# Modulation groups by channel quarter, and nine instead of six early w_in chunks, in the first stage of a two-block kernel

## What is computed

```python
def adaln(cvec, w, b):
    m = jax.nn.silu(cvec) @ w + b
    return jnp.split(m[:, None, :], N_MOD, axis=-1)
...
sh1, sc1, ga1, sh2, sc2, ga2 = adaln(c, w_mod[i], b_mod[i])
csh1, csc1, cga1, csh2, csc2, cga2 = adaln(c_ctx[None, :], w_mod[i], b_mod[i])
px = modulate(rms_norm(x, norm_mix[i]), sh1, sc1) @ w_in[i]
pc = modulate(rms_norm(xc, norm_mix[i]), csh1, csc1) @ w_in[i]
```

## Time and profile before

| | |
|---|---|
| median of three runs | 2884.47 us (2882.27 to 2885.92) |
| profiled execution, span | 2886.6 us (no other time of it is given) |
| PE busy | 2817.8 us, 98% |
| DVE busy | 1865.0 us, 65% |
| ACT busy | 1347.8 us, 47% |
| DMA | 532.30 MB, mean 184 GB/s |
| chain that ended last | PE 90%, DVE 4%, DMA 2%, ACT 1%, issue 1% |

### The profile page before, as it was taken

The page is one execution under the profiler, slowest core; times in us unless marked ns, Lnnn a source line. Parts: engine busy times, 40 slices in busy tenths (PEclk is TensorE's granted clock), DMA queues, the critical chain, the costliest instruction groups (busy, mean ns, idle before and its releaser), DMA issues.

```text
span 2886.6 us, 56801 instructions
## 1 busy us (share of the span) xinstructions
PE 2817.8 (98%) x24171; PEld 2382.1 (83%) x24171; DVE 1865.0 (65%) x2553; ACT 1347.8 (47%) x1947; POOL 226.0 (8%) x271
## 2 busy tenths in 40 slices
PE   6999999999999999999999999999999999999998
PEld 3687888888988878888888888888888888888887
DVE  3597886777777676664455566789775555554444
ACT  3222446566655444444444444566544444444443
POOL 1000002333231000000000000133000000000000
PEclk9999999999999999999999999999999999999999
DMA  9997881000001668876656556666556666666664
GB/s 386 369 373 262 273 274 36 8 11 10 8 8 58 209 211 261 260 236 183 189 185 194 191 180 221 189 178 182 172 182 189 191 188 188 191 189 199 189 191 160
DMA packets 470781, 532.30 MB, mean 184 GB/s; under 512 B 22920, under 2 KB 422722, under 8 KB 469634
## 3 DMA queue, kind: packets, MB, share of 16 engines
q1 hardware_dynamic: 464754, 516.13, 55.6%
q0 software_dynamic: 3408, 10.43, 1.1%
q10 hardware_dynamic: 2368, 2.11, 0.3%
HBM read 522.29 MB, written 4.19 MB: 182 GB/s over the span
## 4 chain that ended last, share of the span: by engine, by line
PE 90%; DVE 4%; DMA 2%; ACT 1%; issue 1%; ACTq 0%; SPq 0%; DVEq 0%
PE ps L2489 14%; PE ps L2500 14%; PE ps L2502 14%; PE ps L2501 14%; PE ps L2665 9%; PE ps L2490 7%; PE ps L3015 4%; PE ps L3016 2%; PE ps L2511 2%; PE ps L2512 2%; PE ps L2513 2%; DMA raw<-in_w_mod 1%; PE ps L2693 1%; PE ps L2691 1%; PE ps L2912 1%
## 5 line engine op out<-in xcount | busy, mean ns | idle before, releaser
L1596 DVE TENSOR_TENSOR lo<-raw,hi 128x1024 fp32r<-128x1024 f32 x776 | 948.5, 1228 | 714.7 <-ACT hi L1069 709.4
L1069 ACT ACTIVATE hi<-raw 128x1024 fp32r<-128x1024 f32 x776 | 820.3, 1059 | 1074.1 <-PE ps L2502 603.0
L2500 PE MATMUL ps<-hi,mov 128*128 128x512 f32 x1408 | 553.4, 393 | 3.6 <-DVE mov L1664 3.6
L2502 PE MATMUL ps<-hi,mov 128*128 128x512 f32 x1408 | 549.3, 390 | 0.0
L2501 PE MATMUL ps<-lo,mov 128*128 128x512 f32 x1408 | 549.0, 390 | 0.0
L2500 PEld LDWEIGHTS ps<-hi,mov 128*128 128x128 f32 x1408 | 264.9, 188 | 58.2 <-issue 4.4
L2502 PEld LDWEIGHTS ps<-hi,mov 128*128 128x128 f32 x1408 | 264.9, 188 | 55.9
L2501 PEld LDWEIGHTS ps<-lo,mov 128*128 128x128 f32 x1408 | 265.1, 188 | 53.9
L2489 PE MATMUL ps<-mov,hi 128*128 128x512 f32 x864 | 306.2, 399 | 0.4 <-DVE mov L2419 0.3
L2489 PE MATMUL ps<-hid,hi 128*128 128x512 f32 x704 | 244.3, 394 | 0.0
L2490 PE MATMUL ps<-mov,lo 128*128 128x256 f32 x864 | 242.2, 280 | 0.0
(11 more groups left out here) (448 smaller groups left out, 4248.7 us busy)
## 6 DMA issues: line engine op xcount, KB each, us to landing
raw<-in_w_in SPq DMA_DIRECT2D x184, 512.0 KB, 4.8
raw<-in_w_gate SPq DMA_DIRECT2D x176, 256.0 KB, 2.9
raw<-in_w_up SPq DMA_DIRECT2D x176, 256.0 KB, 3.2
raw<-in_w_down SPq DMA_DIRECT2D x88, 512.0 KB, 3.6
raw<-in_w_ffn_gate SPq DMA_DIRECT2D x176, 256.0 KB, 2.9
raw<-in_w_ffn_up SPq DMA_DIRECT2D x176, 256.0 KB, 3.1
raw<-in_w_ffn_down SPq DMA_DIRECT2D x88, 512.0 KB, 4.4
raw<-in_w_out SPq DMA_DIRECT2D x64, 512.0 KB, 4.0
```

What stands on the lines that cost most here:

```text
L1069: act.activation(hi[:, s, :, :], src, ACT.Copy).then_inc(hi_ready, 1)
L1596: dve.tensor_tensor(lo[:, s, :, :], raw_at(ph, i, j)[0], hi[:, s, :, :].bitcast(F32), ALU.subtract)\
L2500: pe.matmul(out, x(k)[:, 0, tokens], w_hi, start=first, stop=False)
L2502: mm = pe.matmul(out, x(k)[:, 1, tokens], w_hi, start=False, stop=last)
```

## The change

Each modulation group now holds shift and scale of one channel quarter: a load has two runs of 512 columns instead of one of 1024. `mod_add` adds both parts and forms the gains in each group, so `mod_ready` counts four additions per group. After group m, DVE scales the eight operands of quarter m, and ACT and DVE make their high and low parts. The early part of in_kv goes by chunk first, then by pair, so that mains 3m to 3m+2 need quarter m alone. Nine mains are early: eight among the modulation chunks (behind chunks 21 to 58), the ninth behind the last. The turns of x and ctx stand one per chunk. The loads use a list `MOD_FIRST` of twenty places, in which the later `side_hid` region serves too, and then the fourteen buffers of the ring in another order. Sides are moved from the first trip of in_kv to in_r, and the twenty of its second trip now stand behind seven mains instead of eight.

```diff
 MOD_CHUNKS = MODS * KB
-MODS_READY = 2 * MODS
-EARLY_MAINS = 6
+MOD_PARTS = 2
+MODS_READY = 2 * MOD_PARTS * MODS
+QUARTER = KB // MODS
+EARLY_MAINS = 9
-SIDES = {"in_kv": (4, 20, 20, 20), "in_lora": (8,), "in_r": (4, 4), "in_rest": (6, 6, 4, 0), "ffn": (2,) + (6,) * 5 + (0,) * 5}
+SIDES = {"in_kv": (0, 20, 20, 20), "in_lora": (8,), "in_r": (6, 6), "in_rest": (6, 6, 4, 0), "ffn": (2,) + (6,) * 5 + (0,) * 5}
...
-            self.order = [(p, c) for cs in ((0, 1), (2, 3)) for p in range(EARLY_PAIR + 1) for c in cs]
+            self.order = [(p, c) for c in range(n) for p in range(EARLY_PAIR + 1)]
...
-            first = EARLY_MAINS if (name, i) == ("in_kv", 0) else 0
             steps = 16 if name == "ffn" else 8
+            first = min(max(EARLY_MAINS - 8 * i, 0), steps) if name == "in_kv" else 0
...
-    TURNED_AT = {1 + 3 * m // 2: m for m in range(KB)}
+    TURNED_AT = {1 + m: m for m in range(KB)}
-    COLUMNS_AT = {KB + 1: 0, 2 * KB - 1: 1, 3 * KB + 1: 2, MOD_CHUNKS - 1: 3}
-    MAINS_AT = {35: 0, 40: 1, 46: 2, 52: 3, 57: 4}
-    RING_UPTO = 27
-    MOD_RING = [SIDE_R, SIDE_R + 1, *range(SPARE, SPARE + 4), *range(MOD_KV, MOD_KV + 8)]
-    MAIN_LOADS_AT = {29: (0,), 36: (1,), 41: (2,), 46: (3,), 51: (4,), 56: (5,)}
+    COLUMNS_AT = {KB + 1: 0, 2 * KB + 1: 1, 3 * KB + 1: 2, MOD_CHUNKS - 1: 3}
+    MAINS_AT = {21: 0, 27: 1, 33: 2, 37: 3, 43: 4, 49: 5, 53: 6, 58: 7}
+    MOD_FIRST = [*range(2 * RING), *range(SIDE_HID, SIDE_HID + 4), *range(SPARE, SPARE + 4), *range(SIDE_HID, SIDE_HID + 4)]
+    MOD_RING = [SIDE_R, SIDE_R + 1, *range(MOD_KV, MOD_KV + 8), *range(SPARE, SPARE + 4)]
+    MAIN_LOADS_AT = {12: (0,), 17: (1,), 23: (2,), 28: (3,), 33: (4,), 39: (5,), 44: (6,), 49: (7,), 54: (8,)}
+
+    MAIN_SPLITS = ((1, 2), (3, 4, 5), (6, 7, 8), (9, 10))
...
-                sp.dma_start(tile, A["w_mod"][k * P:(k + 1) * P, ds(part * D + first * P, WIDE)]).then_inc(raw_in[c.buffer], 16)
+                src = A["w_mod"][k * P:(k + 1) * P, 0:MOD_PARTS * D].rearrange("p (a n) -> p a n", a=MOD_PARTS)
+                sp.dma_start(tile.rearrange("p (a n) -> p a n", a=MOD_PARTS), src[:, :, g * QUARTER * P:(g + 1) * QUARTER * P])\
+                  .then_inc(raw_in[c.buffer], 16)
...
             split(PH["in_kv"], 0, 0)
-            act.wait_ge(mod_ready, 2 * 2)
-            for g in range(4):
-                first_hi(g)
-                if g == 3:
-                    split(PH["in_kv"], 0, 1)
-            for main in range(2, EARLY_MAINS):
-                split(PH["in_kv"], 0, main)
-            act.wait_ge(mod_ready, MODS_READY)
-            for g in range(4, 8):
...
+            for m in range(MODS):
+                act.wait_ge(mod_ready, 2 * MOD_PARTS * (m + 1))
+                for g in (2 * m, 2 * m + 1):
+                    if g >= 6:
+                        act.wait_ge(mov_ready, 8 * (g - 4))
+                    first_hi(g)
+                for main in MAIN_SPLITS[m]:
+                    split(PH["in_kv"], 0, main)
...
-            def first_scaled(half):
-                for n in range(half * KB, (half + 1) * KB):
+            def first_scaled(m):
+                for n in range(2 * QUARTER * m, 2 * QUARTER * (m + 1)):
...
+                for part in (1, 0):
+                    for q in range(2):
+                        dve.tensor_tensor(blocks(modcol(part, q, first, QUARTER)),
+                                          ps[:, 5, 0:2 * KB // 2].rearrange("p (h n q) -> p q n h", h=2, q=2)[:, q, 2 * part:2 * part + 2],
+                                          blocks(vcol("b_mod", part * KB + first, QUARTER)), ALU.add).then_inc(mod_ready, 1)
+                dve.wait_ge(mod_ready, 2 * MOD_PARTS * g + 2)
...
-            split(PH["in_kv"], 0, 0)
-            dve.wait_ge(mod_ready, 2 * 2)
-            for g in range(4):
-                first_lo(g)
...
+            for m in range(MODS):
+                mod_row(m)
+                mod_add(m)
+                dve.wait_ge(gain_ready, 2 * m + 2)
+                if m == 0:
                     dve.wait_ge(factor_ready, 1)
                     dve.wait_ge(x_out, KB // 2)
                     dve.wait_ge(ctx_out, KB // 2)
-                    first_scaled(0)
...
+                first_scaled(m)
+                if m == 0:
+                    split(PH["in_kv"], 0, 0)
+                for g in (2 * m, 2 * m + 1):
+                    first_lo(g)
+                for main in MAIN_SPLITS[m]:
+                    split(PH["in_kv"], 0, main)
```

More of the change, by code:

```diff
@@ L731, in all_chunks @@
         for j in range(MOD_CHUNKS):
-            buffer = j % (2 * RING) if j <= RING_UPTO else MOD_RING[(j - RING_UPTO - 1) % len(MOD_RING)]
+            n = j - len(MOD_FIRST)
+            buffer = MOD_FIRST[j] if n < 0 else MOD_RING[n % len(MOD_RING)]
             load, raw_free = placed(buffer)
+            if SIDE_HID <= buffer < MOD_KV:
+                raw_free = released.get(buffer)
             mods.append(Chunk(buffer, load, 0, 0, raw_free, []))
             released[buffer] = mod_used, j + 1
+        for buffer in range(SIDE_HID, MOD_KV):
+            del released[buffer]
         for ph in order:
@@ L1121, in _ @@
                 act.activation(c4[:, :, 2 * q:2 * q + 1], csil[:, q, :], ACT.Copy).then_inc(chi_ready, 1)
-            for j in range(MOD_CHUNKS):
+            for j in range(KB + 2):
                 if j in SQUARE_AT:
@@ L1704, in mod_add @@
             def mod_add(g):
-                part, first = mod_part(g)
+                first = QUARTER * g
                 dve.wait_ge(vec_ready, 1)
@@ L1708, in mod_add @@
                 blocks = lambda x: x.rearrange("p (n h) -> p n h", h=2)
-                for q in range(2):
-                    dve.tensor_tensor(blocks(modcol(part, q, first, KB // 2)),
-                                      ps[:, 5, 0:2 * KB // 2].rearrange("p (h n q) -> p q n h", h=2, q=2)[:, q],
-                                      blocks(vcol("b_mod", part * KB + first, KB // 2)), ALU.add).then_inc(mod_ready, 1)
-                if part == 1:
-                    dve.wait_ge(mod_ready, 2 * g + 2)
-                    for q in range(2):
-                        dve.scalar_tensor_tensor(out=gain[:, q, first:first + KB // 2], in0=modcol(1, q, first, KB // 2), scalar=1.0,
-                                                 in1=vcol("norm_mix", first, KB // 2), op0=ALU.add, op1=ALU.mult).then_inc(gain_ready, 1)
+                for part in (1, 0):
[4 more added lines that the diff above has]
+                dve.wait_ge(mod_ready, 2 * MOD_PARTS * g + 2)
+                for q in range(2):
+                    dve.scalar_tensor_tensor(out=gain[:, q, first:first + QUARTER], in0=modcol(1, q, first, QUARTER), scalar=1.0,
+                                             in1=vcol("norm_mix", first, QUARTER), op0=ALU.add, op1=ALU.mult).then_inc(gain_ready, 1)
             def gains(n, part, q, norm):
@@ L1728, in first_lo @@
                                              in1=mov1[:, ds(k, 1), 0, 1 - q, :].bitcast(F32), op0=ALU.add, op1=ALU.subtract).then_inc(mov_ready, 1)
-            for j in range(2 * KB):
-                if j % KB == KB - 1:
-                    mod_row(j // KB)
+            for j in range(KB + 2):
                 if j in TURNED_AT and TURNED_AT[j] % 2 == 0:
@@ L1747, in _ @@
                     dve.wait_ge(ctx_out, KB // 2)
-                    first_scaled(0)
-            split(PH["in_kv"], 0, 0)
-            dve.wait_ge(mod_ready, 2 * 2)
-            for g in range(4):
-                first_lo(g)
-                if g == 3:
-                    split(PH["in_kv"], 0, 1)
-            for main in (2, 3):
-                split(PH["in_kv"], 0, main)
-            mod_row(2)
-            mod_add(2)
-            dve.wait_ge(gain_ready, 4)
-            first_scaled(1)
-            for main in range(4, EARLY_MAINS):
-                split(PH["in_kv"], 0, main)
-            mod_row(3)
-            mod_add(3)
-            dve.wait_ge(mod_ready, MODS_READY)
-            for g in range(4, 8):
-                first_lo(g)
-                if g in (5, 6):
-                    split(PH["in_kv"], 0, EARLY_MAINS + g - 5)
+                first_scaled(m)
[5 more added lines that the diff above has]
+                    split(PH["in_kv"], 0, main)
             def mod_sides(at):
```

18 lines of the change are left out of this document (4 added, 14 removed).

## The result

The changed kernel took 2891.45 us in the median of 17 runs (2888.69 to 2895.52) beside 2884.47 us for the kernel before: a ratio of 1.0022, 95% interval 1.0015 to 1.0029. That is 7.0 us by the medians and 4.3 to 8.4 us by the interval; 5.9 us, to 2890.4, were forecast. The profiled execution took 2890.58 us, its span is 2888.6.

A forecast was written before the change was run, and what follows sets the result against it. TensorE was taken as nearly full from 66 us, losing 5.9 us to DVE waits and clock; -1.9 + 3.2 + 1.7 + 7.1 + 1.7 - 5.9 = +5.9 us gave 2890.4 us, range 2880.5 to 2899.

The forecast's parts named there:

- front, by main 8: From the start to main 8: main 0 earlier, less added work and waits; main 8 near 125.8, 1.9 us gained.
- gap before main 9: Ahead of main 9, TensorE free at 131.3 waits for the last quarter's operands until 134.5: 3.2 us lost.
- lower clock at main 9: Behind the wait ahead of main 9, matmuls run at the lower clock level: 1.7 us lost.
- gap before main 12: TensorE waits after main 11 until DVE, with eight sides in between, has emptied pair 1: 7.1 us lost.
- lower clock at main 12: Behind the wait ahead of main 12, matmuls run at the lower clock level: 1.7 us lost.
- losses of the kernel before: Between mains 5 and 14 of the kernel before, waits for DVE's lows and lower clock cost 5.9 us, subtracted.
- Main 0: First main among the chunks: operands, ending later than the data, let it start at 52.8, 13.6 us earlier.
- rival of the held clock: At mains 0, 9 and 12 the clock doesn't fall, 1.7 us each: +0.8, 2885.3 us; chance 0.15.
- the late load: Main 12's load stands in SP's queue behind sides 6 and 7, which reuse buffers: +14.6, 2899 us; chance 0.12.
- Main 12 isn't held: Pair 1 is empty when TensorE ends main 11, so 8.8 us go: -2.9, 2881.6 us; chance 0.15.
- The sides in in_r and the ring of loads: Four sides moved to in_r: nothing, or 4.8 us if TensorE's cover failed; new buffer order of the loads: nothing.
- mains at the lower clock among chunks: Mains 0 to 2 all run at 0.43 us a matmul: +18.6, 2903 us; chance 0.05.

The follow-up runs named there:

- early_operands: Changed kernel with main 9's split ahead of the last group's operands and mains waiting block by block; 2886.76 us, ratio 1.0011 to the kernel before.
- own_buffers: Changed kernel with sides 6 and 7 loaded into two buffers of their own; 2889.21 us, ratio 1.0022 to the kernel before.
- later_sides: Changed kernel with DVE taking two sides behind pair 0's taps and nine behind pair 1's; 2895.96 us, ratio 1.0046 to the kernel before.
- early_and_loads_ahead: early_operands with loads of mains 10, 11 and a spill issued before the first sides, later mains two places earlier; 2879.82 us, ratio 0.9994 to the kernel before.

## Why the prediction was right

It was right in sign and size, and in the cause that it forecast, DVE's order; it held a second lock beside it to be unlikely. The terms, at the start of main 14:

| term | predicted | in the profile after |
|---|---|---|
| front, by main 8 | -1.9 | -2.5 |
| gap before main 9 | +3.2 | +3.0 |
| lower clock at main 9 | +1.7 | +0.15 |
| gap before main 12 | +7.1 | +7.75 |
| lower clock at main 12 | +1.7 | +2.8 |
| losses of the kernel before | -5.9 | -5.9 |
| sum | +5.9 | +5.3 |

That the sum came within 0.6 us is in part luck. The clock took 1.5 us less at main 9 and 1.1 more at main 12 than reckoned, the front and the gap before main 12 were each off by 0.6, and these errors nearly cancel.

- **Main 0** was laid out to 52.8 and came at 53.03, and the waits ahead of mains 3 and 6 were 0.84 each against 1.15. The four additions of a group cost next to nothing (0.37 us at 125.39, against 0.24 for two in the earlier trace rows). That the operands, and not the data, set the front held: a 5% faster load moved main 0 by 0.5. The front scatters: with the same first stage, main 8 came between 124.60 and 126.20 in seven profiles.
- **The gap before main 9** came as reckoned, ended by DVE's low half. Its price for the clock did not come in this profile, and did in two others (below). Of the three places of the rival of the held clock, it was thus right at main 9 alone: behind the waits ahead of mains 0 and 12 matmuls stood 0.43 apart.
- **The gap before main 12** was reckoned through DVE's order alone, and the eight sides took 8.6 us where 8.5 were reckoned. What the prediction had as a rival, the late load, was there at the same time and equally long: it ended 0.25 us behind the backlog. It was priced at 14.6 us, by a load of 14 us; it took 5.91, and its further price was next to nothing. So DVE's order alone gives the gap to within 0.25 us. "Main 12 isn't held" would have needed both locks open.
- **What the sum doesn't tell**: a term is what was lost, not what an edit gives back. The gap before main 12 and its clock, 10.5 us together, did come back when the sides moved (9.6 us, counted from main 9's start), where the rival of the free main 12 had 8.8. The others did not come back alone: without the gap before main 9 main 12 stood still (10.46 us of wait), with one lock open it stood still, and without the lower clock at main 12 a later load and DVE's work took back all but 0.3 us, where the rival of the held clock had 1.7 for each place.
- **The sides in in_r and the ring of loads** were set at nothing. The profile pair is 5.1 to 5.7 us apart from main 14 up to 480 us, which leaves at most a few tenths for the sides. The ring works ahead of main 0, which came 0.2 us behind its forecast. No run tried either alone.
- The rivals of mains at the lower clock among chunks (granted 1.00 from 66 to 111 us) and of a change without effect (main 0 at 53) are out for this kernel. In a run with an earlier front (early_operands) the first of them did come, at one main.

## What to carry to other kernels

When a reordering makes several accumulations end together, look at what the engine that empties them does between the first and the second, and whether the same engine idles just before: the work was cheap there and dear ten microseconds later. A wait's named releaser is only the last of those who came late; before pricing an edit, follow the second latest too, here a load behind a buffer's reuse in an in-order queue. A sum of waits tells what a change costs, not what removing one of them returns.

## What was not expected of the hardware

- The same wait had two outcomes. Eight profiles have a wait of 2.68 to 2.70 us ahead of main 9; in six main 10 followed after 5.57 to 5.61 us, in two (own_buffers and later_sides) after 7.1, with matmuls at 0.43. A wait of 1.98 ahead of main 12 was followed by seven slow matmuls, one of 2.63 in another run by none (main 13 after 5.60). The three waits for data ahead of main 2 were followed by thirteen slow matmuls in early_operands (waits of 0.46 to 0.80 us) and by none in early_and_loads_ahead (0.41 to 0.81). So the length of the wait alone does not tell whether the clock falls; what does stays open. From main 9 on, all waits of 4.19 us or more were followed by slow matmuls.
- Two runs of 2 KB per partition cost 5% of the load rate against one of 4 KB (380 against 399 GB/s, in one stretch of one pair of profiles).
- A load that is issued behind a block of others can land 14 us later, as main 11's did in early_operands (issued 126.09, used 140.19), where main 12's took 5.91 in the changed kernel; and the wait shows at ACT, two engines away from the queue that caused it.
